# One fp32 copy of the turned probabilities, and fp32 values on two halves of the tensor engine

## The reference

```
s = einsum('bqhd,bkhd->bhqk', q, k) * SCALE + (q_cum - k_cum)
p = masked_softmax(s, k_pos <= q_pos)
o = einsum('bhqk,bkhd->bqhd', p, v)
```

## Time and profile before

| | us |
|---|---|
| median of three runs | 2063.82 (2063.62 to 2071.12) |
| the profiled execution | 2058.45 |
| its span, first to last instruction | 2056.7 |
| PE busy over the span | 1857.6 (90%) |
| DVE / ACT / POOL busy | 1006.2 / 733.1 / 542.6 |
| main attention, about 742 to 1138 | 396 |

### The profile page before, as it was taken

One profiled execution on the slowest core, in us unless ns is written; L12 is line 12 of the kernel. 1 busy time (PEld: TensorE's weight loads), 2 busy tenths in 40 slices (PEclk: granted clock), 3 DMA queues, 4 the chain that ended last, 5 costly groups with the idle time before them and its releaser, 6 DMA issues. The chain is left out here.

```text
span 2056.7 us, 31665 instructions
## 1 busy us (share of the span) xinstructions
PE 1857.6 (90%) x11624; PEld 1628.5 (79%) x11624; DVE 1006.2 (49%) x1899; ACT 733.1 (36%) x1456; POOL 542.6 (26%) x626
## 2 busy tenths in 40 slices
PE   2988999998877889999998798999999999799995
PEld 2888877997644778778777686999999999776674
DVE  2323421333333557777777652333323232466997
ACT  2223411212322157777777431211111111133352
POOL 4310022421453422222211201112211221143452
PEclk9899999999998579999999899999999999899998
DMA  6452343356987943322221122111111111164533
GB/s 148 87 113 108 133 157 122 115 165 204 315 260 231 229 135 75 66 62 62 63 51 58 75 82 71 42 41 46 55 42 41 43 55 54 37 217 141 189 130 134
DMA packets 168965, 229.21 MB, mean 111 GB/s; under 512 B 44716, under 2 KB 113125, under 8 KB 168711
## 3 DMA queue, kind: packets, MB, share of 16 engines
q1 hardware_dynamic: 144282, 154.58, 25.0%
q0 software_dynamic: 24560, 73.03, 12.8%
HBM read 192.59 MB, written 40.18 MB: 113 GB/s over the span
## 5 line engine op out<-in xcount | busy, mean ns | idle before, releaser
L121 PE MATMUL gate_acc<-o_T_hi,w_gate_split_hi 128*128 128x352 f32 x528 | 171.6, 325 | 2.3 <-ACTq L2696 2.3
L121 PE MATMUL up_acc<-o_T_hi,w_up_split_hi 128*128 128x352 f32 x528 | 170.4, 323 | 0.7 <-DVEq L2739 0.7
L122 PE MATMUL gate_acc<-o_T_lo,w_gate_split_hi 128*128 128x352 f32 x528 | 170.3, 323 | 0.0
L123 PE MATMUL gate_acc<-o_T_hi,w_gate_split_lo 128*128 128x352 f32 x528 | 170.2, 322 | 0.0
L122 PE MATMUL up_acc<-o_T_lo,w_up_split_hi 128*128 128x352 f32 x528 | 169.2, 321 | 0.0
L123 PE MATMUL up_acc<-o_T_hi,w_up_split_lo 128*128 128x352 f32 x528 | 169.1, 320 | 0.0
L2324 DVE TENSOR_TENSOR pa_probs_T_lo<-pa_t,pa_probs_T_hi 128x512 fp32r<-128x512 f32 (+3 forms) x288 | 145.6, 528 | 38.6 <-ACT pa_probs_T_hi L2253 37.3
L2177 PE MATMUL pa_t<-ident,pa_scores 128*128 128x128 f32 x816 | 138.5, 275 | 24.8 <-DVE pa_probs_T_lo L2324 23.9
L2253 ACT ACTIVATE pa_probs_T_hi<-pa_t 128x512 fp32r<-128x512 f32 (+3 forms) x288 | 130.9, 473 | 80.1 <-PE pa_t L2177 74.5
L2238 ACT ACTIVATE pa_scores<-pa_scores,pa_neg_max 128x128 f32<-128x128 f32 (+1 forms) x192 | 143.5, 747 | 16.2 <-DVE pa_neg_max L2276 12.6
L121 PE MATMUL y_acc<-w_down_split_hi,act_split_hi 128*128 128x512 f32 x308 | 125.4, 407 | 19.0 <-DVE act_split_lo L3061 19.0
(11 more groups left out here) (441 smaller groups left out, 4765.5 us busy)
## 6 DMA issues: line engine op xcount, KB each, us to landing
w_down_raw<-in_w_down SPq DMA_DIRECT2D x59, 512.0 KB, 4.3
fox_k_pages<-in_cache_fox_kv SPq DMA_DIRECT2D x64, 256.0 KB, 6.3
w_rows<-in_cache_fox_kv POOLq DMA_DIRECT2D x48, 256.0 KB, 8.1
w_gate<-in_w_gu SPq DMA_DIRECT2D x22, 512.0 KB, 3.7
w_up<-in_w_gu SPq DMA_DIRECT2D x22, 512.0 KB, 3.7
w_rows<-in_w_in SPq DMA_DIRECT2D x5, 2048.0 KB, 10.5
sel_pages<-in_cache_nsa_kv POOLq DMA_DIRECT2D x64, 128.0 KB, 7.5
pa_k_fox<-scratch_kf_d POOLq DMA_DIRECT2D x32, 256.0 KB, 6.3
```

Of the source, the lines that this page charges most:

```text
L121: pe.matmul(out, a[0][at], b[0][bt], start=start, stop=False)
L122: pe.matmul(out, a[0][at], b[1][bt], start=False, stop=False)
L123: return pe.matmul(out, a[1][at], b[0][bt], start=False, stop=stop)
```

## The change

In the main attention the turned probabilities are no longer split: `pa_probs_T` is one fp32 tile, even chunks are copied by ACT alone and odd chunks by DVE alone, each freeing its own PSUM tile. The values stay as they are loaded (fp32, 64 columns), so `split_values` and the raw buffers go, and the loads write straight into `pa_v_*`. A value matmul is now one fp32 matmul for each key tile, with a stationary operand of 64 columns. Key tiles alternate between the two halves of PE's columns: even ones write PSUM partitions 0 to 63 and odd ones 64 to 127, and L2286 adds the two halves as it added the two parts. The values of a pair are issued as one block, after the chunks of unit s-2, and no longer in pieces between the chunks. Counts on the semaphore of the values double, since the last matmul on each half increments it.

```diff
-        self.v = {kind: [ph.sb(f"pa_v_{kind}{u}", [P, NT, 2, HD], FR) for u in range(2)] for kind in kinds}
-        self.v_raw = [ph.sb(f"pa_v_raw{u}", [P, NT, HD]) for u in range(2)]
+        self.v = {kind: [ph.sb(f"pa_v_{kind}{u}", [P, NT, HD]) for u in range(2)] for kind in kinds}
...
-                if n >= 2:
-                    sp.wait_ge(pa.s_gs, n - 1)
...
-        pT = [split(ph, f"pa_probs_T{i}", [P, NT + 1, 2, P]) for i in range(2)]
+        pT = [ph.sb(f"pa_probs_T{i}", [P, NT + 1, 2, P]) for i in range(2)]
...
                 if n >= 2:
-                    pe.wait_ge(s_cd, n - 1)
+                    pe.wait_ge((s_ca, s_cd)[n % 2], n // 2)
...
-                for y in range(begin, end):
-                    slot, key = mine[y // 2]
-                    ins = pe.matmul(O[p % 2][:, 0:2 * P], v[kind][u][:, key, :, :].rearrange("p w e -> p (w e)"),
-                                    pT[p % 2][y % 2][:, slot, :, :].rearrange("p a n -> p (a n)"),
-                                    start=y == 0, stop=y == n - 1)
+                for y, (slot, key) in enumerate(mine):
+                    side = y % 2 * HD
+                    ins = pe.matmul(O[p % 2][side:side + HD, 0:2 * P], v[kind][u][:, key, :],
+                                    pT[p % 2][:, slot, :, :].rearrange("p a n -> p (a n)"), start=y < 2, stop=y >= n - 2)
...
-                    for n in now[side]:
-                        turn(n)
-                        if live:
-                            values(p, x / rounds, (x + 1) / rounds)
-                        x += 1
+                    if 0 <= s - 2 + side < NU:
+                        for n in of_unit[s - 2 + side]:
+                            turn(n)
+                    if side == 0 and 0 <= p < NPR:
+                        values(p)
...
+                        if n % 2 == 0:
...
+                            act.activation(pT[p % 2][:, slot:slot + m, e % 2, :], PT[0][:, 0:m * P].rearrange("p (m n) -> p m n", n=P),
+                                           ACT.Copy).then_inc(s_ca, 1)
...
-                        dve.wait_ge(s_ca, n + 1)
-                        dve.tensor_tensor(lo, PT[n % 2][:, 0:m * P].rearrange("p (m n) -> p m n", n=P), hi, ALU.subtract).then_inc(s_cd, 1)
+                        if n % 2 == 1:
+                            dve.wait_ge(s_t, n + 2)
+                            dve.tensor_copy(pT[e // 2 % 2][:, slot:slot + m, e % 2, :],
+                                            PT[1][:, 0:m * P].rearrange("p (m n) -> p m n", n=P)).then_inc(s_cd, 1)
```

More of the change, by code:

```diff
@@ L1867, in _ @@
                             pool.dma_start(pa.k[kind][u][w_][r * HD:(r + 1) * HD, :], d[src][w_, u]).then_inc(pa.s_kl[u], 16)
[L1868 to L1873, removed]
         @block.tensor
@@ L2095, in _ @@
         def _(pool):
[L2096 to L2099, removed]
+            for t in pT:
+                for slot, half in ((0, 0), (NT, 1)):
+                    pool.tensor_copy(t[:, slot, half, :], c.zero[:, :].to_broadcast([P, P])).then_inc(s_z, 1)
             pool.sem_inc(s_mg, 2)
@@ L2178, in turn, with values @@
                 ins.then_inc(s_t, 1)
-            def values(p, begin, end):
+            def values(p):
                 i, j, t = units[2 * p]
@@ L2183, in values @@
                 mine = pair_slots(p)
[L2184 to L2194, removed]
-                for y in range(begin, end):
-                    slot, key = mine[y // 2]
-                    ins = pe.matmul(O[p % 2][:, 0:2 * P], v[kind][u][:, key, :, :].rearrange("p w e -> p (w e)"),
-                                    pT[p % 2][y % 2][:, slot, :, :].rearrange("p a n -> p (a n)"),
-                                    start=y == 0, stop=y == n - 1)
-                    if y == n - 1:
+                n = len(mine)
+                last = of_unit[2 * p + 1][-1]
+                pe.wait_ge(s_ca, last // 2 + 1)
+                pe.wait_ge(s_cd, (last + 1) // 2)
+                if p == 0:
+                    pe.wait_ge(s_z, 4)
+                if t == 0 and kind == "fox":
+                    pe.wait_ge(pa.s_fv[u], 16 * i + 16)
+                if t == 0 and kind != "fox":
+                    pe.wait_ge(pa.s_gv[2 * u + (kind == "win")], 16)
+                pe.wait_ge(s_n, max(1, p))
+                for y, (slot, key) in enumerate(mine):
+                    side = y % 2 * HD
+                    ins = pe.matmul(O[p % 2][side:side + HD, 0:2 * P], v[kind][u][:, key, :],
+                                    pT[p % 2][:, slot, :, :].rearrange("p a n -> p (a n)"), start=y < 2, stop=y >= n - 2)
+                    if y >= n - 2:
                         ins.then_inc(s_o, 1)
@@ L2241, in _ @@
                     p = (s - 6) // 2
-                    act.wait_ge(s_o, p + 2)
+                    act.wait_ge(s_o, done(p))
                     act.wait_ge(s_bk, max(0, p - 1) + 1)
@@ L2247, in _ @@
                     p = e // 2
[L2248 removed]
+                    act.wait_ge(s_o, done(p - 2))
                     for n in of_unit[e]:
[L2250 to L2254 removed]
+                        if n % 2 == 0:
+                            _, a, m = chunks[n]
+                            slot = slots(e)[a][1]
+                            act.wait_ge(s_t, n + 2)
+                            act.activation(pT[p % 2][:, slot:slot + m, e % 2, :], PT[0][:, 0:m * P].rearrange("p (m n) -> p m n", n=P),
+                                           ACT.Copy).then_inc(s_ca, 1)
         @block.vector
@@ L2318, in _ @@
                     e = s - 2
+                    dve.wait_ge(s_o, done(e // 2 - 2))
                     for n in of_unit[e]:
-                        _, a, m = chunks[n]
-                        slot = slots(e)[a][1]
-                        hi, lo = (pT[e // 2 % 2][w_][:, slot:slot + m, e % 2, :] for w_ in range(2))
-                        dve.wait_ge(s_ca, n + 1)
-                        dve.tensor_tensor(lo, PT[n % 2][:, 0:m * P].rearrange("p (m n) -> p m n", n=P), hi, ALU.subtract).then_inc(s_cd, 1)
+                        if n % 2 == 1:
+                            _, a, m = chunks[n]
+                            slot = slots(e)[a][1]
+                            dve.wait_ge(s_t, n + 2)
+                            dve.tensor_copy(pT[e // 2 % 2][:, slot:slot + m, e % 2, :],
+                                            PT[1][:, 0:m * P].rearrange("p (m n) -> p m n", n=P)).then_inc(s_cd, 1)
 def output_and_norm(c, oT, wo, gate):
```

34 lines of the change are left out of this document (6 added, 28 removed).

## The result

The changed kernel takes 2081.3 us (median of 7 runs, 2075.4 to 2090.0) against 2064.0 (2060.8 to 2072.0) on the same chip: ratio 1.0075, 95% interval 1.0051 to 1.0099. That is 17 us slower; 2078 was forecast.

The account below looks back on a forecast made before the run. PE bounds the main attention (busy 359 of 396 us). 23 us more PE work with waits about as long; following jobs gave +17, taken as +15: 2064 + 15 = 2079, stated as 2078; range 2042 to 2102.

Parts of the forecast that it names:

- Value matmuls: Main attention on PE: 464 fp32 matmuls on two halves side by side cost 101 us, against 111 us before.
- D: Rival for the value matmuls: the halves do not work side by side, +129 us, 2207 us; chance 0.04.
- The switch: PE going into and out of the half-column shape once for each of 96 pairs: 0.34 us each, 33 us.
- full drain: PE draining wholly at each change of shape: 0.07 us more for each way in, 7 us.
- B: Rival: the change of shape on PE costs nothing, so 33 us of the sum go, 2046 us; chance 0.10.
- The waits: PE's waits for copies in the main attention: about as long as before, only in other places; 53 us in all.
- the four rounds: PE's four rounds of a sel job, eight units: forecast 4.81, 4.01, 3.46 and 5.08 us, 17.36 against 16.54 before.
- A: Rival: PE's waits for copies go, leaving a quarter of 53 us; -25 us, 2039 us; chance 0.16.
- C: Rival: odd copies push each other back and half as much again is lost in waits, 2105 us; chance 0.10.
- The walk: Following PE step by step through sel, win and fox jobs: +2.1 us for three jobs, 8 times, +17 us.
- granted clock: Sign for the main attention: if its clock fell below 1.00, none of the sums would hold.
- Record starts 0.11 apart: Sign of being right: value matmuls stand in blocks on PE with their records starting 0.11 us apart.

Follow-up runs that it names:

- late block: The changed kernel with each pair's value block behind the odd unit's chunks instead of the even unit's: 2040.0 us, ratio 0.9879 to the kernel before.
- the pieces: The changed kernel with each pair's values in pieces between the transposed chunks, as before the change: 2136.9 us, ratio 1.0357 to the kernel before.
- two-block kernel: The changed kernel with each pair's values in two halves, behind the even and the odd unit's chunks: 2089.8 us, ratio 1.0135 to the kernel before.
- whole-width blocks: The changed kernel with value matmuls on PE's whole width, two neighbouring key tiles as 128 columns: 2155.2 us, ratio 1.0434 to the kernel before.

## Why the prediction was right

**Value matmuls, 101 us forecast.** Right: 464 x 0.216 = 100, side by side, so D is out. (One after the other they would have cost 464 x 0.43 = 200, not the 230 of the prediction, which scaled matmuls of 64 moving columns up to 256.)

**The switch, 0.34 us a block, 33 us.** Right. Where nothing else waits, it is 0.35: in the late block's rows six transposes start at 911.92 and the values at 912.66, 0.19 after the last one instead of 0.11; its four tiles last until 913.68, 1.02 where 0.86 are their slots; and the scores take 0.35 to 914.03 instead of 0.24. That is 0.08 + 0.16 + 0.11.

```profile
911.92 0.82 PE L2157 MATMUL pa_t<-ident,pa_scores 128*128 128x128 f32 x6
...
912.66 1.08 PE L2177 MATMUL pa_o<-pa_probs_T,pa_v_sel 128*64 128x256 f32 x8
...
913.68 0.51 PE L2141 MATMUL pa_s<-pa_k_win,pa_q_nsa 128*128 128x256 f32 x2
...
914.03 0.93 PE L2157 MATMUL pa_t<-ident,pa_scores 128*128 128x128 f32 x7
```

That is 34 us for 96 blocks, and the pieces, with 287 of them, come out with it. The two balances of whole kernels give less, 0.28 and 0.25: the two-block kernel still has short waits, and whole-width blocks seem to have a small price of their own. The prediction's rows from another stage had given the right size. The 0.07 that it reckoned for a full drain would have made 0.41 a block; 0.35 was measured. B (nothing) is out.

**The waits, about as long as before.** Right, nearly. Start to start, the four rounds lost 0.63 + 0.24, 0.18 + 0.30, 0.36 and 0.45 us, 2.16 in all (forecast 0.55 + 0.28, 0.11 + 0.42, 0.39, 0.59: 2.34). For 24 jobs that is 52 us, near the 55 of the table and the 53 that the prediction took. Before the change 62 us were lost. A (the waits go) and C (more is lost) are both out; but the experiments show that A was one index away: with another place for the block 42 of the 55 us go, and the copies are the same.

**The sum.** By the table, matmuls -11.2, switches +33.6 and waits -6.9 make the +15.5, where +23 of work was forecast. The walk had given 6 us less in waits (+17), and 2 more were taken off for small losses, for which there was no row. For three jobs the walk gave +2.1 us and the trace +2.1 (51.0 against a mean of 48.9). The sel and win jobs came out at 17.23 and 16.98 (17.36, 17.0), fox at 16.76, 0.26 longer than the 16.5 that I gave it without writing its rounds out. Value loads, POOL's splits and fills were forecast at nothing; no run tried them apart. The granted clock of 0.99 (a sign named in the prediction was a clock below 1.00) changes nothing: in both profiles the first 4 us of the stage are at the lower level, 0.50, and the rest is at 1.00. "Record starts 0.11 apart", a sign I had named, shows as two within 0.01 and then a step of 0.2 or so; the mean is the same.

## What to carry to other kernels

Against values split in two on the whole width, two column halves pay only when the block between the switches is long: here one switch (0.35 us) eats what some fifteen tiles save (0.24 - 0.216 each), and no block has more than eight; splitting such a block, above all into odd parts, adds to the loss. Against unsplit fp32 on the whole width they save 76 us of this stage, switches included, and unsplit values are what lets one copy of the probabilities do. The change paid only once the block stood in the right place, and that place alone gave the kernel before 4 us at most: follow each PSUM buffer round the loop, and put the longest independent block between the last chunk that fills the buffers and the next that needs them. Price a bundle by its parts: by the table the block's first place cost 32 us (62 to 94), the single copies gave back 39 (94 to 55), and the halves cost 22 (33.6 - 11.2); changing one index then turned +17 us into -24.

## What the runs showed of the hardware

- PE runs ahead across column halves, but not far: two matmuls on one half and then two on the other take no longer than in turn; three and three cost 0.48 us more, four and four 0.88.
- Single fp32 matmuls of 256 columns take 0.43 us on one half (a one-tile piece is as long as two tiles, 0.58) or on the whole width (two records each, 0.216 from start to start); on two halves in turn they take 0.216 each. Two matmuls of the split, rounded values take 0.24.
- A block on two halves between full-width work costs 0.35 us more than its matmuls: 0.08 on the way in, 0.16 in the block, 0.11 on the first scores behind it.
- PE's idle time in the profile is less than what its waits cost: 32 us shown and about 55 lost in the changed kernel (an estimate from dense steps), 4 and 13 with the late block.
